# Norms on ScalarE alone: Exp of minus half a Ln in place of Sqrt and a VectorE reciprocal

## Chip, core and metric

One core of a Trainium2 chip. The metric is the device time of one execution in microseconds, the median of several runs.

## What is computed

Two layers of a hybrid trunk on 256 tokens (128 of a context and 128 of a sample), width 1024, all in fp32. Layer 0 is a Mamba-2 SSD mixer beside grouped attention, layer 1 a gated linear attention (GLA). Behind each mixer comes a mixture of 16 experts (top group, then top 2 in it). Five RMS norms stand ahead of mixers and experts and at the end, one more in the SSD mixer, and one per head in the GLA mixer:

```python
def rms_norm(x, w):
    xf = x.astype(F32)
    y = xf * lax.rsqrt(jnp.mean(xf * xf, axis=-1, keepdims=True) + EPS)
    return (y * w.astype(F32)).astype(x.dtype)
# layer: x += gate * mixer(modulate(rms_norm(x)));  x += gate * moe(modulate(rms_norm(x)))
# SSD: y = rms_norm(y * silu(z), norm_w);   GLA: y = rms_norm(y_f + y_b, norm_w) * silu(r), 256 channels a head
```

## The kernel before

Each engine has its own program, and all order between them is by semaphores written out by hand. Activations lie transposed: features on the 128 partitions, 8 tiles (KT), by 256 tokens (T). SyncE streams some 290 MB of weights in tiles of 1 MB through 6 ring slots, and 12 slots in the expert stages; `slot_used` frees them in the order of their use. TensorE multiplies tile by tile; its fp32 matmuls appear in the trace as two instructions each. Banks of PSUM (`ps`) are reused by hand.

A main norm, `norm(i)` for i = 0 to 4, runs so: ScalarE squares the 8 tiles into `hT` (L923); TensorE sums them over the features with a matrix of 1/1024 into bank 0 (semaphore `ss`); ScalarE takes the root with epsilon as bias into `rstd` (L926, semaphore `rms`); VectorE inverts it (L1176) and scales 16 half tiles (L1185, or 8 whole tiles at L1181 for i = 4); ScalarE adds the shift to each (L935), and TensorE starts on the first tiles as they come. norm(0) also needs the first modulation row, which ScalarE copies (L916) once eight weight tiles have been used.

The SSD norm: ScalarE squares the gated result (L997); TensorE sums it into bank 0; ScalarE takes the root (L999, `yrms`). TensorE waits for `yrms` before it writes attention scores over bank 0, with three matmuls for the rotary embedding (`C(ROT)`) between. VectorE's part (`ssd_norm`, L1277 and eight times L1279) comes later, between the maxima of the second group of scores (L1305 to L1313) and the normalising of its exponentials (L1321), which ScalarE computes meanwhile (L1008, L1010).

The GLA norm: ScalarE squares (L1063); TensorE sums per head into banks 4 and 5 (`gss` after each bank, two heads a bank); ScalarE takes the root of each bank, 128x512 (L1066, `grms`); VectorE inverts one head at a time (L1407), scales (L1408) and gates (L1409, `gyn`) its two tiles. The output projection on TensorE waits for both banks' `grms` and for each tile's `gyn`.

ScalarE evaluates its functions from tables, and the build puts an ACT_TABLE_LOAD ahead of an activation whose function the active table lacks. Such loads are in no line of the source: they carry the line of the activation that follows. Square, Copy and Identity need none. Where an activation has one wait, the wait is the activation's own, and the load ahead of it does not wait; where it has two (L926: `set_up` and `ss`), the load waits for `ss`. Other functions around the norms: Exp and Ln for dt (L940, L943), Exp of the segments (L983), Exp of the softmax (L1008), Exp in the router (L1070, L1072), Silu in projections and experts (L1038, L1094).

```python
act.wait_ge(S("ss"), i + 1)
act.activation(rstd[:, 0, :], ps[:, 0, 0:T], ACT.Sqrt, bias=eps[:, :]).then_inc(S("rms"), 1)
# VectorE
dve.wait_ge(S("rms"), i + 1)
step(dve.reciprocal(rstd[:, 0, :], rstd[:, 0, :]))
```

Of the kernel before, what the change touches and what calls it, by code (L numbers as in the profile page):

```python
# [19 lines left out]
ACT = mybir.ActivationFunctionType  # L20
# [6 lines left out]
T = 256  # L27
# [15 lines left out]
PER_EXPERT = 6  # L43
# [58 lines left out]
def build(nc, A, O):  # L102
    with ExitStack() as ctx:
# [21 lines left out]
        rstd = sb("rstd", [P, GH, T])  # L125
# [20 lines left out]
        eps = sb("eps", [P, 1])  # L146
# [114 lines left out]
        def _(sp):  # L261
# [24 lines left out]
            for l in range(2):  # L286
                for j in range(len(IN[l])):
                    w_in_load(l, j)
                    for c in ada_after(l, j):
                        ada(3 * l + 1 + c // KT, c % KT)  # L290
                for j in range(n_out[l]):
                    if l == 0:
                        ada(3, j)
                    n = pos["out", l, j]
                    wait_free(n)
                    load(n, w_out[l][256 * j:256 * j + 256, :].rearrange("(k p) n -> p k n", p=P), 2)
                base = pos["moe", l]
                wgu = [A[w][l].rearrange("e (p k) f -> p e k f", p=P) for w in ("w_gate_exp", "w_up_exp")]
                wd = A["w_down_exp"][l].rearrange("e (p j k) d -> p e j k d", p=P, k=2)

                def expert(e, c, n):

                    if c < 4:
                        src = wgu[c // 2][:, bass.ds(e, 1), 4 * (c % 2):4 * (c % 2) + 4, :]
                        return slot(n, 4), src.rearrange("p a k f -> p (a k) f")
                    src = wd[:, bass.ds(e, 1), c - 4, :, :]
                    return slot(n, 2), src.rearrange("p a k d -> p (a k) d")

                for n, (a, c) in enumerate(PAIR_ORDER):
                    wait_free(base + n)  # L310
                    if n == 0:
                        sp.wait_ge(*((S("gy_raw"), 2) if l else (S("att_raw"), 3)))
                    if MOE_SLOT[n] == RING + 4:
                        sp.wait_ge(*((S("gyn"), KT) if l else (S("slot_used"), pos["out", 0, KT // 2 - 1] + 1)))
                    if MOE_SLOT[n] == RING + 5:
                        sp.wait_ge(S("slot_used"), pos["out", l, n_out[l] - 1] + 1)
                    dst, src = expert(a, c, base + n)
                    sp.dma_start(dst, src).then_inc(S(f"landed{home[base + n]}"), 16)
                with sp.Fori(1, PAIRS) as i:
                    for n, (a, c) in enumerate(PAIR_ORDER):  # L320
                        sp.wait_ge(S("slot_used"), i * (2 * PER_EXPERT) + (base + n + 1 - 2 * PER_EXPERT))
                        dst, src = expert(i * 2 + a, c, base + n)
                        sp.dma_start(dst, src).then_inc(S(f"landed{home[base + n]}"), 16)

                sp.wait_ge(S("need"), l + 1)
                most = sp.value_load(need[0:1, l:l + 1], min_val=0, max_val=T)
                with sp.If(most > CAP):
                    sp.wait_ge(S("slot_used"), base + NE * PER_EXPERT)
                    with sp.Fori(0, NE) as e:
                        with sp.Fori(1, T // CAP) as r:  # L330
                            it = e * (T // CAP - 1) + r
                            for c in range(PER_EXPERT):

                                sp.wait_ge(S(f"o{l}_used"), it * PER_EXPERT + (c + 1 - PER_EXPERT))
                                dst, src = expert(e, c, c)
                                assert home[c] == c
                                sp.dma_start(dst, src).then_inc(S(f"o{l}_landed{c}"), 16)

                    sp.wait_ge(S(f"o{l}_used"), (NE * (T // CAP - 1) + 1) * PER_EXPERT)
            for s in range(NS):  # L340
# [58 lines left out]
        def _(pe):  # L399
# [302 lines left out]
            def moe(l):  # L702
# [123 lines left out]
                with pe.If(most > CAP):  # L826
                    pe.sem_inc(S(f"o{l}_used"), PER_EXPERT)
                    with pe.Fori(0, NE) as e:
                        with pe.Fori(1, T // CAP) as r:
                            it = e * (T // CAP - 1) + r  # L830

                            def wait(n):
                                pe.wait_ge(S(f"o{l}_landed{n}"), it * 16)

                            def mark(ins):
                                ins.then_inc(S(f"o{l}_used"), 1)
                            pe.wait_ge(S(f"o{l}_v"), it * O_STEPS + (1 - O_STEPS))
                            for k in range(KT):
                                for s in range(NS):
                                    last = mm(pe, ps[:, 0, k * CAP:(k + 1) * CAP], xtok[:, s, k * P:(k + 1) * P],  # L840
                                              O_DISP[:, s * CAP:(s + 1) * CAP], s == 0, s == 1)
                            last.then_inc(S(f"o{l}_p"), 1)
                            for s in range(NS):
                                last = mm(pe, ps[0:CAP, 1, tk(s)], O_DISW[:, s * CAP:(s + 1) * CAP], C(IDENT), True, True)
                            last.then_inc(S(f"o{l}_p"), 1)
                            pe.wait_ge(S(f"o{l}_v"), it * O_STEPS + (3 - O_STEPS))
                            gate_or_up(2, [O_HG], 0, wait, mark)
                            gate_or_up(3, [O_HG], 2, wait, mark)
                            pe.wait_ge(S(f"o{l}_v"), it * O_STEPS + (4 - O_STEPS))
                            for f in range(FT):  # L850
                                last = mm(pe, ps[:, 1, f * CAP:(f + 1) * CAP], O_ACT[:, f * P:(f + 1) * P], cst[0:CAP, IDENT, 0:CAP], True, True)
                            last.then_inc(S(f"o{l}_p"), 1)
                            pe.wait_ge(S(f"o{l}_v"), it * O_STEPS + (5 - O_STEPS))
                            down(2, [O_HT], 4, wait, mark)
                            pe.wait_ge(S(f"o{l}_v"), it * O_STEPS)
                            for m in range(KT):
                                last = mm(pe, ps[:, 4 + m // 2, (m % 2) * T:(m % 2 + 1) * T], O_YS[:, m * P:(m + 1) * P],
                                          O_CT, False, False, shared=True)
                            last.then_inc(S(f"o{l}_p"), 1)
# [24 lines left out]
        def _(act):  # L884
# [33 lines left out]
            def norm(i):  # L918
# [4 lines left out]
                    act.activation(hT[:, k, :], xT[:, k, :], ACT.Square).then_inc(S("sq"), 1)  # L923
                act.wait_ge(S("set_up"), 1)
                act.wait_ge(S("ss"), i + 1)
                act.activation(rstd[:, 0, :], ps[:, 0, 0:T], ACT.Sqrt, bias=eps[:, :]).then_inc(S("rms"), 1)  # L926
                if i == 0:
                    ada_copy(0)
                if i < 4:
# [7 lines left out]
            def even():  # L937
# [58 lines left out]
                act.wait_ge(S("y_gated"), 2)  # L996
                act.activation(W(4), zsf, ACT.Square).then_inc(S("ysq"), 1)  # L997
                act.wait_ge(S("yss"), 1)
                act.activation(rstd[:, 1, :], ps[:, 0, 0:T], ACT.Sqrt, bias=eps[:, :]).then_inc(S("yrms"), 1)  # L999
                for g in range(3):  # L1000
                    nh, w = (8, 256) if g else (16, 128)
                    act.wait_ge(S("negm"), g + 1)
# [21 lines left out]
            def odd():  # L1024
# [38 lines left out]
                act.activation(W(3), yaf, ACT.Square).then_inc(S("gsq"), 1)  # L1063
                for b in range(2):
                    act.wait_ge(S("gss"), b + 1)
                    act.activation(rstd[:, 2 * b:2 * b + 2, :].rearrange("p h t -> p (h t)"), ps[:, 4 + b, :], ACT.Sqrt, bias=eps[:, :]).then_inc(S("grms"), 1)  # L1066

            def moe(l):
                act.wait_ge(S("g_sub"), l + 1)
# [63 lines left out]
        def _(dve):  # L1133
# [38 lines left out]
                    step(scales(l, *((8, NMIX) if t == 0 else (32, NFFN))))  # L1172

            def norm(i):
                dve.wait_ge(S("rms"), i + 1)
                step(dve.reciprocal(rstd[:, 0, :], rstd[:, 0, :]))  # L1176
                if i == 0:
                    ada_done(0)
                for k in range(KT):
# [21 lines left out]
            def even():  # L1201
# [72 lines left out]
                    tt(zs[:, :, tk(s)], zs[:, :, tk(s)], xbc[:, 0:KT, tk(s)], ALU.mult).then_inc(S("y_gated"), 1)  # L1274
                def ssd_norm():
                    dve.wait_ge(S("yrms"), 1)
                    step(dve.reciprocal(rstd[:, 1, :], rstd[:, 1, :]))  # L1277
                    for k in range(KT):
                        last = stt(zs[:, k, :], zs[:, k, :], feat[:, SSDN + k:SSDN + k + 1], rstd[:, 1, :], ALU.mult, ALU.mult)  # L1279
                        if k < KT - 1:  # L1280
                            step(last)
                    last.then_inc(S("yssd"), 1)
# [53 lines left out]
            def odd():  # L1336
# [65 lines left out]
                    dve.tensor_copy(yatt[:, :, tk(s)], ps[:, 2 * s:2 * s + 2, :].rearrange("p b (k t) -> p (b k) t", k=4)).then_inc(S("gy"), 1)  # L1402
                dve.wait_ge(S("proj_free"), 28)
                for i in range(KT):
                    if i % 2 == 0:
                        dve.wait_ge(S("grms"), i // 4 + 1)
                        step(dve.reciprocal(rstd[:, i // 2, :], rstd[:, i // 2, :]))  # L1407
                    step(stt(yatt[:, i, :], yatt[:, i, :], feat[:, GLAN + i % 2:GLAN + i % 2 + 1], rstd[:, i // 2, :], ALU.mult, ALU.mult))  # L1408
                    tt(yatt[:, i, :], yatt[:, i, :], zs[:, i, :], ALU.mult).then_inc(S("gyn"), 1)  # L1409
                dve.wait_ge(S("slot_used"), pos["out", 1, n_out[1] - 1] + 1)  # L1410
# [163 lines left out]
```

## Time and profile before

| | |
|---|---|
| median of 3 runs | 1195.73 us (1193.99 to 1200.53) |
| profiled execution | 1196.1 us, its span 1194.0 us |
| TensorE busy | 1036.6 us (87%), mean granted clock 0.917 |
| VectorE busy | 269.9 us (23%) |
| ScalarE busy | 198.6 us (17%) |
| data moved by DMA | 302.84 MB |

Times in the rows are microseconds from the start of the span. Busy time of an engine says how much it works, the chain of waits what the end waited for. An idle stretch in brackets, with the name behind the arrow, says how long the engine stood still before an instruction and what released it. The granted clock is a share of full speed: 1.00 is 2.4 GHz, 0.50 is 1.2 GHz.

### The profile page before, as it was taken

The numbers are of one execution on the slowest core, as the hardware profiler recorded it, in microseconds if no ns is written. First come the engines' busy times: TensorE is split into PE (matmuls) and PEld (weight loads), VectorE is DVE, ScalarE is ACT, GpSimd is POOL, SyncE is SP. The second block draws the span as 40 slices with busy tenths as digits, with TensorE's granted clock in tenths as the row PEclk, the third lists the DMA queues.
The fourth block names the chain that finished last, engine by engine and source line by source line (L and its number), as shares of the span: only waits on it lengthen the run. The fifth ranks groups of instructions, "written<-read, shape, count | busy, mean of one in ns | idle before, by whom it ended". The sixth has DMA issues, their size and how long they took to land.

```text
span 1194.0 us, 12914 instructions
## 1 busy us (share of the span) xinstructions
PE 1036.6 (87%) x5318; PEld 662.9 (56%) x5318; DVE 269.9 (23%) x531; ACT 198.6 (17%) x402; POOL 33.4 (3%) x34
## 2 busy tenths in 40 slices
PE   0799998773399789999999799978988899999995
PEld 0477776453377554455554377746976545555433
DVE  0346003735400430010000400037144310010003
ACT  0310213323200420000000300122013200010002
POOL 5000101200000000000000000000000000000000
PEclk9789999987699879999999899987588899999998
DMA  9758775100057719999999558831037199999980
GB/s 306 276 192 273 254 259 209 36 1 1 0 183 311 282 41 423 421 422 422 422 422 415 194 199 310 289 135 36 1 141 282 71 423 421 422 422 422 422 351 36
DMA packets 75521, 302.84 MB, mean 254 GB/s; under 512 B 5261, under 2 KB 40855, under 8 KB 44759
## 3 DMA queue, kind: packets, MB, share of 16 engines
q1 hardware_dynamic: 67232, 294.67, 63.2%
q10 hardware_dynamic: 7479, 6.74, 1.7%
q0 software_dynamic: 768, 0.83, 0.4%
q8 instruction: 32, 0.52, 0.2%
q14 instruction: 10, 0.08, 0.0%
HBM read 298.81 MB, written 3.41 MB: 253 GB/s over the span
## 4 chain that ended last, share of the span: by engine, by line
PE 82%; DVE 8%; ACT 3%; DMA 2%; issue 2%; POOL 1%; ACTq 0%; POOLq 0%; DVEq 0%
PE ps L255 79%; PE ps L404 3%; DMA xtok<-in_x_sample_dram 2%; ACT wide L1008 1%; ACT hT L935 1%; POOL mix L393 1%; DVE rstd L1176 1%; DVE tiny L1305 1%; DMA ring<-in_w_ada_dram 1%; ACTq L886 0%; DVE wide L1476 0%; DVE wide L1474 0%; DVE mix L1279 0%; DVE wide L1330 0%; ACT L926 0%
## 5 line engine op out<-in xcount | busy, mean ns | idle before, releaser
L255 PE MATMUL ps<-ring,wide 128*64 128x512 f32 x768 | 171.3, 594 | 1.5 <-ACT wide L1098 1.5
L255 PE MATMUL ps<-mix,wide 128*64 128x512 f32 x768 | 168.0, 592 | 0.0
L255 PE MATMUL ps<-hT,ring 128*128 128x256 f32 x640 | 146.2, 387 | 0.0
L255 PEld LDWEIGHTS ps<-hT,ring 128*128 128x128 f32 x640 | 122.1, 193 | 30.1 <-ACT mix L954 6.7
L255 PEld LDWEIGHTS ps<-mix,wide 128*64 128x64 f32 x768 | 55.0, 137 | 108.8 <-issue 108.8
L255 PEld LDWEIGHTS ps<-ring,wide 128*64 128x64 f32 x768 | 54.0, 137 | 107.1 <-issue 105.2
L255 PE MATMUL ps<-wide 128*128 (+4 forms) x512 | 87.4, 344 | 6.9 <-DVE wide L1265 3.3
L255 PE MATMUL ps<-mix,ring 128*128 128x256 f32 x384 | 85.3, 381 | 1.0 <-DVE mix L1409 1.0
L255 PEld LDWEIGHTS ps<-wide 128*128 128x128 f32 (+1 forms) x512 | 74.6, 194 | 16.3 <-DVE wide L1265 4.1
L255 PEld LDWEIGHTS ps<-mix,ring 128*128 128x128 f32 x384 | 72.2, 190 | 17.5 <-issue 8.1
L255 PEld LDWEIGHTS ps<-wide,xtok 128*128 128x128 f32 x512 | 63.7, 206 | 18.3 <-issue 11.4
L255 PE MATMUL ps<-wide,xtok 128*128 (+1 forms) x512 | 66.8, 293 | 6.3 <-DVE wide L1476 6.3
L1496 DVE TENSOR_TENSOR wide<-wide,ps 128x512 f32<-128x512 f32 x16 | 16.8, 1052 | 213.3 <-PE ps L255 213.3
L255 PE MATMUL ps<-ring,hT 128*128 128x256 f32 x256 | 57.4, 382 | 0.0
L404 PE MATMUL ps<-cst,wide 128*128 128x128 f32 x172 | 27.7, 312 | 32.4 <-DVE wide L1325 29.8
L255 PEld LDWEIGHTS ps<-ring,hT 128*128 128x128 f32 x256 | 48.0, 190 | 12.9 <-issue 1.7
L255 PE MATMUL ps<-ring,csilu 128*32 128x512 f32 x384 | 50.2, 612 | 2.9 <-DMA ring<-in_w_ada_dram 2.2
L1488 DVE COPY wide<-ps 128x512 f32<-128x512 f32 x16 | 11.1, 691 | 160.9 <-PE ps L255 160.9
L1166 DVE TENSOR_TENSOR mods<-ps,feat 128x32 f32<-128x32 f32 x6 | 1.1, 190 | 193.1 <-PE ps L404 193.1
L404 PEld LDWEIGHTS ps<-cst,wide 128*128 128x128 f32 x172 | 23.7, 164 | 35.1 <-issue 24.0
L1194 DVE SCALAR_TENSOR_TENSOR xT<-ps,mods,xT 128x128 f32<-128x128 f32 x64 | 19.9, 347 | 97.5 <-PE ps L255 86.0
L1081 ACT ACTIVATE wide<-ps 128x512 f32<-128x512 f32 x16 | 9.6, 597 | 155.9 <-PE ps L255 155.9
(230 smaller groups left out, 830.2 us busy)
## 6 DMA issues: line engine op xcount, KB each, us to landing
mix<-in_w_gate_exp_dram SPq DMA_DIRECT2D x64, 1024.0 KB, 14.4
ring<-in_w_up_exp_dram SPq DMA_DIRECT2D x64, 1024.0 KB, 17.5
ring<-in_w_ada_dram SPq DMA_DIRECT2D x48, 1024.0 KB, 7.4
ring<-in_w_down_exp_dram SPq DMA_DIRECT2D x32, 1024.0 KB, 12.5
mix<-in_w_down_exp_dram SPq DMA_DIRECT2D x32, 1024.0 KB, 14.7
ring<-in_w_in_even_dram SPq DMA_DIRECT2D x16, 1024.0 KB, 6.0
ring<-in_w_in_odd_dram SPq DMA_DIRECT2D x12, 1024.0 KB, 7.9
ring<-in_w_out_even_dram SPq DMA_DIRECT2D x8, 1024.0 KB, 5.6
```

What stands on the lines that cost most here:

```text
L255: return pe.matmul(out, lhsT, rhs, start=first, stop=last, skip_group_check=shared)
L393: pool.tensor_tensor(heads(U), C(GE if n % 2 else LE)[:, None, :].broadcast_to([P, HEADS, P]), tiny[:, a0:a0 + 16][:, :, None].broadcast_t ...
L404: return pe.transpose(out, in_, cst[0:n, IDENT, 0:n])
L935: act.activation(hT[:, k, tk(s)], hT[:, k, tk(s)], ACT.Identity, bias=mods[:, l, c + k, s:s + 1]).then_inc(S("h_ready"), 1)
L1008: act.activation(pr[:, h, :], sc[:, h, :], ACT.Exp, scale=SCALE, bias=tiny[:, NEGM + h:NEGM + h + 1], accum_out=tiny[:, RSUM + h:RSUM + h ...
L1081: act.activation(W(1)[:, 0:512], ps[:, 0, :], ACT.Copy).then_inc(S("hg"), 1)
L1166: tt(mods[:, l, 16 * t:16 * t + 16, :].rearrange("p (j b) s -> p j b s", b=4), ps[:, ADA_TURN[third], :].rearrange("p (b j r) -> p j b r", ...
L1176: step(dve.reciprocal(rstd[:, 0, :], rstd[:, 0, :]))
L1194: last = stt(xT[:, k, tk(s)], ps[:, 4 + k // 2, (k % 2) * T + s * P:(k % 2) * T + (s + 1) * P], mods[:, l, c + k, s:s + 1], xT[:, k, tk(s) ...
L1305: step(dve.tensor_reduce(tiny[:, MX:MX + nh], sc, AX.X, ALU.max))
L1488: dve.tensor_copy(YS[:, 512:1024], ps[:, 1, :]).then_inc(S("ys"), 1)
L1496: tt(HACT.rearrange("p (f a) -> p a f", f=FT), SIL.rearrange("p (a f) -> p a f", f=FT), ps[:, 3, :].rearrange("p (a f) -> p a f", f=FT), A ...
```

## The change

In each norm the root becomes a Ln of the same input with the same bias, and a second activation, Exp with scale -0.5, gives the inverse root; VectorE's reciprocals go (10 of them). Exp waits for Ln by a semaphore (`rms` itself, `yln`, `gln`). What other engines wait for (`rms`, `yrms`, `grms`) is set by Exp. In the GLA norm the second bank's Ln comes after the first bank's Exp. Apart from the norms, the branch for experts with more than 64 tokens waits on one semaphore for its six weight tiles in place of six.

```diff
--- before.py
+++ after.py
@@ -334,7 +334,7 @@
                                 sp.wait_ge(S(f"o{l}_used"), it * PER_EXPERT + (c + 1 - PER_EXPERT))
                                 dst, src = expert(e, c, c)
                                 assert home[c] == c
-                                sp.dma_start(dst, src).then_inc(S(f"o{l}_landed{c}"), 16)
+                                sp.dma_start(dst, src).then_inc(S(f"o{l}_landed"), 16)
 
                     sp.wait_ge(S(f"o{l}_used"), (NE * (T // CAP - 1) + 1) * PER_EXPERT)
             for s in range(NS):
@@ -830,7 +830,8 @@
                             it = e * (T // CAP - 1) + r
 
                             def wait(n):
-                                pe.wait_ge(S(f"o{l}_landed{n}"), it * 16)
+                                if n == 0:
+                                    pe.wait_ge(S(f"o{l}_landed"), it * (16 * PER_EXPERT))
 
                             def mark(ins):
                                 ins.then_inc(S(f"o{l}_used"), 1)
@@ -923,7 +924,9 @@
                     act.activation(hT[:, k, :], xT[:, k, :], ACT.Square).then_inc(S("sq"), 1)
                 act.wait_ge(S("set_up"), 1)
                 act.wait_ge(S("ss"), i + 1)
-                act.activation(rstd[:, 0, :], ps[:, 0, 0:T], ACT.Sqrt, bias=eps[:, :]).then_inc(S("rms"), 1)
+                act.activation(rstd[:, 1, :], ps[:, 0, 0:T], ACT.Ln, bias=eps[:, :]).then_inc(S("rms"), 1)
+                act.wait_ge(S("rms"), 2 * i + 1)
+                act.activation(rstd[:, 0, :], rstd[:, 1, :], ACT.Exp, scale=-0.5).then_inc(S("rms"), 1)
                 if i == 0:
                     ada_copy(0)
                 if i < 4:
@@ -996,7 +999,9 @@
                 act.wait_ge(S("y_gated"), 2)
                 act.activation(W(4), zsf, ACT.Square).then_inc(S("ysq"), 1)
                 act.wait_ge(S("yss"), 1)
-                act.activation(rstd[:, 1, :], ps[:, 0, 0:T], ACT.Sqrt, bias=eps[:, :]).then_inc(S("yrms"), 1)
+                act.activation(rstd[:, 2, :], ps[:, 0, 0:T], ACT.Ln, bias=eps[:, :]).then_inc(S("yln"), 1)
+                act.wait_ge(S("yln"), 1)
+                act.activation(rstd[:, 1, :], rstd[:, 2, :], ACT.Exp, scale=-0.5).then_inc(S("yrms"), 1)
                 for g in range(3):
                     nh, w = (8, 256) if g else (16, 128)
                     act.wait_ge(S("negm"), g + 1)
@@ -1063,7 +1068,10 @@
                 act.activation(W(3), yaf, ACT.Square).then_inc(S("gsq"), 1)
                 for b in range(2):
                     act.wait_ge(S("gss"), b + 1)
-                    act.activation(rstd[:, 2 * b:2 * b + 2, :].rearrange("p h t -> p (h t)"), ps[:, 4 + b, :], ACT.Sqrt, bias=eps[:, :]).then_inc(S("grms"), 1)
+                    two = rstd[:, 2 * b:2 * b + 2, :].rearrange("p h t -> p (h t)")
+                    act.activation(two, ps[:, 4 + b, :], ACT.Ln, bias=eps[:, :]).then_inc(S("gln"), 1)
+                    act.wait_ge(S("gln"), b + 1)
+                    act.activation(two, two, ACT.Exp, scale=-0.5).then_inc(S("grms"), 1)
 
             def moe(l):
                 act.wait_ge(S("g_sub"), l + 1)
@@ -1172,8 +1180,7 @@
                     step(scales(l, *((8, NMIX) if t == 0 else (32, NFFN))))
 
             def norm(i):
-                dve.wait_ge(S("rms"), i + 1)
-                step(dve.reciprocal(rstd[:, 0, :], rstd[:, 0, :]))
+                dve.wait_ge(S("rms"), 2 * (i + 1))
                 if i == 0:
                     ada_done(0)
                 for k in range(KT):
@@ -1274,7 +1281,6 @@
                     tt(zs[:, :, tk(s)], zs[:, :, tk(s)], xbc[:, 0:KT, tk(s)], ALU.mult).then_inc(S("y_gated"), 1)
                 def ssd_norm():
                     dve.wait_ge(S("yrms"), 1)
-                    step(dve.reciprocal(rstd[:, 1, :], rstd[:, 1, :]))
                     for k in range(KT):
                         last = stt(zs[:, k, :], zs[:, k, :], feat[:, SSDN + k:SSDN + k + 1], rstd[:, 1, :], ALU.mult, ALU.mult)
                         if k < KT - 1:
@@ -1402,9 +1408,7 @@
                     dve.tensor_copy(yatt[:, :, tk(s)], ps[:, 2 * s:2 * s + 2, :].rearrange("p b (k t) -> p (b k) t", k=4)).then_inc(S("gy"), 1)
                 dve.wait_ge(S("proj_free"), 28)
                 for i in range(KT):
-                    if i % 2 == 0:
-                        dve.wait_ge(S("grms"), i // 4 + 1)
-                        step(dve.reciprocal(rstd[:, i // 2, :], rstd[:, i // 2, :]))
+                    dve.wait_ge(S("grms"), i // 4 + 1)
                     step(stt(yatt[:, i, :], yatt[:, i, :], feat[:, GLAN + i % 2:GLAN + i % 2 + 1], rstd[:, i // 2, :], ALU.mult, ALU.mult))
                     tt(yatt[:, i, :], yatt[:, i, :], zs[:, i, :], ALU.mult).then_inc(S("gyn"), 1)
                 dve.wait_ge(S("slot_used"), pos["out", 1, n_out[1] - 1] + 1)
```

The changed order on ScalarE, with the table loads that the build puts in. First norm(1), ahead of the first expert stage. Before:

```order
L923 ACTIVATE hT<-xT 128x256 x8
L926 ACT_TABLE_LOAD
L926 ACTIVATE rstd<-ps,eps 128x256
L935 ACTIVATE hT<-hT,mods 128x128 x16
L1070 ACT_TABLE_LOAD
L1070 ACTIVATE tiny<-tiny 128x8
L1072 ACTIVATE tiny<-tiny 128x8
```

Now:

```order
L924 ACTIVATE hT<-xT 128x256 x8
L927 ACT_TABLE_LOAD
L927 ACTIVATE rstd<-ps,eps 128x256
L929 ACT_TABLE_LOAD
L929 ACTIVATE rstd<-rstd 128x256
L938 ACTIVATE hT<-hT,mods 128x128 x16
L1078 ACTIVATE tiny<-tiny 128x8
L1080 ACTIVATE tiny<-tiny 128x8
```

The load ahead of the router's Exp (L1070) has moved into the norm, between Ln and Exp.

Next the GLA norm, ScalarE, with the semaphores that are waited for. Before:

```order
L1060 DMA out_dram<-hT 128x4x256 [waits state]
L1060 DMA out_dram<-hT 128x4x256
L1063 ACTIVATE wide<-mix 128x2048 [waits gy]
L1066 ACT_TABLE_LOAD
L1066 ACTIVATE rstd<-ps,eps 128x512 [waits gss] x2
```

Now:

```order
L1068 ACTIVATE wide<-mix 128x2048 [waits gy]
L1072 ACT_TABLE_LOAD
L1072 ACTIVATE rstd<-ps,eps 128x512 [waits gss]
L1074 ACT_TABLE_LOAD
L1074 ACTIVATE rstd<-rstd 128x512 [waits gln]
L1072 ACT_TABLE_LOAD
L1072 ACTIVATE rstd<-ps,eps 128x512 [waits gss]
L1074 ACT_TABLE_LOAD
L1074 ACTIVATE rstd<-rstd 128x512 [waits gln]
```

One load has become four, since the two banks alternate between the functions.

Last, norm(3), which follows the GLA norm on ScalarE. Before:

```order
L1066 ACTIVATE rstd<-ps,eps 128x512 x2
L923 ACTIVATE hT<-xT 128x256 x8
L926 ACTIVATE rstd<-ps,eps 128x256
L935 ACTIVATE hT<-hT,mods 128x128 x16
L1070 ACT_TABLE_LOAD
```

It had no load, because the root's table was active from the GLA norm; now its rows are those shown for norm(1), with two loads. Over the program there are 20 loads before and 26 now.

## Rows read from the trace of the kernel before

**Rows 1.** Page, part 4: the chain that ended last, by engine
```profile
PE 82%; DVE 8%; ACT 3%; DMA 2%; issue 2%; POOL 1%; ACTq 0%; POOLq 0%; DVEq 0%
```
**Rows 2.** The same chain in order of time: start, duration, engine and line
```profile
296.60 1.67 DVE rstd L1277
...
676.48 1.76 DVE rstd L1176
...
1181.59 1.76 DVE rstd L1176
```
**Rows 3.** Timeline, norm(1): start, duration, instructions, idle time before and releaser
```profile
403.24 1.28 ACT L926 ACT_TABLE_LOAD   x1 [0.83 <-PE ps L255]
404.54 0.47 ACT L926 ACTIVATE rstd<-ps,eps 128x256 f32<-128x256 f32 x1
405.11 1.75 DVE L1176 RECIPROCAL rstd<-rstd 128x256 f32<-128x256 f32 x1 [3.15 <-ACT rstd L926]
406.90 5.29 DVE L1185 SCALAR_TENSOR_TENSOR hT<-xT,mods,rstd 128x128 f32<-128x128 f32 x16
```
**Rows 4.** Groups of instructions, ScalarE: busy us, mean ns, idle before
```profile
L923 ACT ACTIVATE hT<-xT 128x256 f32<-128x256 f32 x40 | 15.9, 413 | 64.5 <-DVE xT L1194 54.7 <-DVE xT L1151 9.9
...
L960 ACT ACTIVATE mix<-mix 128x512 f32<-128x512 f32 x6 | 3.7, 624 | 0.0
```
**Rows 5.** Timeline, ScalarE: the awaited copy in norm(0), the router after norm(1)
```profile
49.92 0.60 ACT L916 ACTIVATE ada_row<-ps 128x512 f32<-128x512 f32 x1 [8.74 <-PE ps L255]
...
417.77 0.21 ACT L1070 ACTIVATE tiny<-tiny 128x8 f32<-128x8 f32 x1 [3.55 <-DVE tiny L1429]
```
**Rows 6.** Timeline, SSD norm on ScalarE and the first scores on TensorE
```profile
268.20 0.47 ACT L999 ACTIVATE rstd<-ps,eps 128x256 f32<-128x256 f32 x1 [4.04 <-PE ps L255]
...
268.69 1.28 ACT L1008 ACT_TABLE_LOAD   x1
...
270.67 2.06 PE L255 MATMUL ps<-mix 64*128 64x128 f32 x32
```
**Rows 7.** Timeline, SSD norm on VectorE, beside ScalarE's last exponential
```profile
296.51 1.74 DVE L1277 RECIPROCAL rstd<-rstd 128x256 f32<-128x256 f32 x1
...
298.29 4.13 DVE L1279 SCALAR_TENSOR_TENSOR mix<-mix,feat,rstd 128x256 f32<-128x256 f32 x8
...
300.24 0.24 ACT L1010 ACTIVATE tiny<-tiny 128x8 f32<-128x8 f32 x1
302.34 0.16 DVE L1321 TENSOR_TENSOR tiny<-tiny 128x8 f32<-128x8 f32 x1
```
**Rows 8.** Timeline, GLA norm and the start of its output projection
```profile
867.95 6.50 PE L255 MATMUL ps<-wide,cst 128*128 128x256 f32 x16 [3.26 <-ACT wide L1063]
871.77 0.69 ACT L1066 ACTIVATE rstd<-ps,eps 128x512 f32<-128x512 f32 x1 [2.57 <-PE ps L255]
...
874.35 0.48 DVE L1408 SCALAR_TENSOR_TENSOR mix<-mix,feat,rstd 128x256 f32<-128x256 f32 x1
874.49 0.69 ACT L1066 ACTIVATE rstd<-ps,eps 128x512 f32<-128x512 f32 x1 [2.03 <-PE ps L255]
874.87 0.42 DVE L1409 TENSOR_TENSOR mix<-mix 128x256 f32<-128x256 f32 x1
...
875.44 27.86 PE L255 MATMUL ps<-mix,ring 128*128 128x256 f32 x128 [0.99 <-DVE mix L1409]
```
**Rows 9.** Timeline, norm(3)
```profile
909.89 0.47 ACT L926 ACTIVATE rstd<-ps,eps 128x256 f32<-128x256 f32 x1 [0.85 <-PE ps L255]
...
912.25 5.29 DVE L1185 SCALAR_TENSOR_TENSOR hT<-xT,mods,rstd 128x128 f32<-128x128 f32 x16
```
**Rows 10.** Windows of 2 us: width, busy PE, PEld, DVE, ACT, POOL, clock, DMA
```profile
872.00:874.00 2.00, 2.00 (x7) 1.64 (x6) 1.44 (x1) 0.46 (x1) 0.00 (x0) 0.60 1.04 438
...
910.00:912.00 2.00, 0.00 (x0) 0.00 (x0) 1.54 (x1) 0.36 (x1) 0.00 (x0) 1.00 1.04 438
...
914.00:916.00 2.00, 1.58 (x8) 1.24 (x7) 1.90 (x7) 2.00 (x8) 0.00 (x0) 0.64 1.04 438
```

## The prediction

> **What bounds the kernel now.** I read the chain of waits first: 82% of the span is TensorE, 8% VectorE, 3% ScalarE [rows 1]. So an edit of ScalarE and VectorE work counts only where that chain leaves TensorE. There the chain in order of time names the norms: of the seven places the change touches, the reciprocal of four is seen on the chain in [rows 2] (the SSD norm at 296.60, norm(2) at 676.48, norm(4) at 1181.59) and [rows 3] (norm(1) at 405.11); [rows 8] and [rows 9] show the other two, the GLA norm and norm(3). norm(0) is not there. Then I read the timeline around each norm, since what decides is which wait ends last there.
>
> About 0.5% of this kernel's time, 6 us, is what a measurement can tell from no change.
>
> **The change, part by part.** It takes a DVE reciprocal away (1.75 us for 128x256) and a Sqrt becomes a Ln of the same operands (same duration taken: both are one pass over the same tile). It adds an Exp on ScalarE. The order of the changed kernel shows what the diff does not: Ln and Exp do not share a table, so a load stands ahead of each Exp, and loads rise from 20 to 26.
>
> *One Exp.* The nearest rows are SBUF to SBUF passes: 413 ns for 128x256, 624 ns for 128x512 [rows 4].
>
> *norm(1), norm(2), norm(4).* Before, from the start of the load to the first scaling on VectorE: 403.24 to 406.90, 3.66 us [rows 3]. Now: load 1.28, Ln 0.47, load 1.28, Exp 0.41, with 0.02 between instructions of one engine (404.54 less 403.24 and 1.28) and 0.10 to VectorE (405.11 less 404.54 and 0.47): 3.60. The second load with the Exp costs what the reciprocal cost. Gain 0.06 each, taken as -0.15 for the three. The load of the Exp table that the router needed after norm(1) and norm(3) goes away, at no gain: after it ScalarE sat idle 3.55 us, waiting for VectorE [rows 5]. The same holds for the load ahead of the dt exponential after norm(0); its cover is the projection that runs meanwhile, and without it the gain would be 1.28.
>
> *norm(0).* What TensorE and VectorE wait for there is the copy of the first modulation row at 49.92, ahead of which ScalarE sat idle for 8.74 us behind its root [rows 5]. A load and an Exp, 1.7 us, fit into that: 0. Without that cover it would read like norm(1), -0.06.
>
> *The SSD norm.* ScalarE first. The root's load is already ahead of its wait, the Exp load follows the Ln directly, where it followed the root (268.69 after 268.20 + 0.47), and the Exp ends at 268.69 + 1.28 + 0.02 + 0.41 = 270.40. This is the one place where the semaphore moves past a load that TensorE used to ignore: TensorE may not overwrite bank 0 with scores before it. It starts them at 270.67, after the rotation matmuls [rows 6]. Covered by 0.2 us; were the Exp 0.5 us longer, 0.3 us would show. VectorE then: the reciprocal starts at 296.51, the first of eight scalings at 298.29, and they end at 302.42. Without it they start at 296.51 and end at 300.64. The next wait there is ScalarE's exponentials, which end at 300.48 [rows 7], just before. So the whole 298.29 - 296.51 = 1.78 us is gained: -1.78.
>
> *The GLA norm.* Here the order matters most. The two halves alternate Ln and Exp, so four loads stand where one did, and the first alone is hidden (ScalarE idles 2.57 us after it, until TensorE's sum). The output projection waits for both halves and for the first gated row. Before: the second root ends at 874.49 + 0.69 = 875.18, the row at 875.29, TensorE starts at 875.44 [rows 8]. Now, from 871.77: Ln to 872.46, load to 873.76, Exp (0.62) to 874.40, load to 875.71, Ln to 876.41, load to 877.71, Exp to 878.36, TensorE 0.06 later (as at any ScalarE release) at 878.42. That is +2.98. The four reciprocals that VectorE saves, 7 us, are worth nothing: the rows it feeds are one per 3.5 us of matmuls (27.86/8), and it was ahead before.
>
> *norm(3).* Before, the root found its table still active from the GLA norm: 909.89 to 912.25, 2.36 us [rows 9]. Now the GLA norm leaves Exp active, so both loads are paid, 3.60 us: +1.24.
>
> *TensorE's clock.* The wait ahead of the GLA output projection grows from 1 us to 878.42 - 874.45 = 3.97 us. The nearest row is norm(3), where TensorE was idle from 909.8 to 913.8: the granted clock was 1.00 in the gap and 0.64, then 0.50, in the windows after [rows 10], a fall from 2.4 to 1.2 GHz. A low clock under this very shape costs 6.50 us for 16 matmuls [rows 8], against 16 x 27.86/128 = 3.48 at full clock: 3.0 us for one such stretch. Bounds 0 and 3.0; I take 1.0, nearer the low end, because the fall is not certain and came in norm(3) only after the wait had ended. Norm(3)'s own clock I charge nothing: it is low there already.
>
> The rest of the diff, one semaphore in place of six for the overflow experts, lies in a branch that the traced run does not enter: 0.
>
> **Sum.** -0.15 - 1.78 + 2.98 + 1.24 = +2.29, with the clock +3.3. The profiled execution took 1196.1 (span 1194.0 and 2.1 around it), 0.4 above the median of 1195.7; so 1199.4 for it, and 1199.0 for a median. Shown runs alone reach from 1194.0 to 1200.5.
>
> On the two tables: the changed order has a load between Ln and Exp in every norm. The Trainium skill (ScalarE: Activation LUTs, "Table sets: the hidden batching unit") says that one set holds both exp and ln, so that the pair needs a single load; by it the sum would be 9.1 us lower (rival D). The order of this build does not agree, and I go by the order.
>
> **The rivals.**
> (A) The clock falls in the GLA gap and the projection pays the full 3.0 us or more, or a second stage loses its clock too: 1195.7 + 2.3 + 3.0 = 1201.0, up to 1203 with a second fall of half that. For it: norm(3)'s gap is as long. Against: the clock held at 1.00 through that whole wait.
> (B) Slower, clear of the noise: a load right behind an activation costs more than its row, since the engine would have to empty first. Seven loads on the path stand so (one in each of norms 1 to 4, three in the GLA norm). At one more load's time each, 1.3 us, that is 9.1 us: 1195.7 + 2.3 + 9.1 = 1207. It decides from 0.5 us a load (+3.5, at the 6 us line). Against it: at 268.69 a load began 0.02 us behind a root, and took 1283 ns as everywhere [rows 6]; but no activation there waited right behind it, which leaves a little room. The Trainium skill (ScalarE: Activation LUTs, "What ACT_TABLE_LOAD costs") puts a drain of 1380 ns on top of 1283 ns for each switch; by it this rival would be 9.7 us. The rows at 268.69 and 403.24 to 404.54 show no such drain.
> (C) The clock falls out luckier than in the traced run. It was low until 873 [rows 10], and the 16 matmuls that sum the GLA squares took 6.50 us [rows 8]; at full clock they take 3.48, and the longer wait behind them costs nothing: 1195.7 + 2.3 - 3.0 = 1195.0, or 1196.5 for half of it. Against: nothing in the change bears on the clock there, so it is for single runs rather than for a median.
> (D) The change does not cost what the order says, because Ln and Exp use one table after all: the seven loads that stand between them, or between Exp and the next Ln, on the path go: 1195.7 + 2.3 - 9.1 = 1189. Against it stands the order, which shows those loads in the build.
>
> **How the numbers follow.** Forecast 0.60 (1197.5 to 1201); A 0.18; C 0.15; B 0.05; D 0.02. The range leaves out B, D and the tails of A and C: 1194.5 to 1204. Slower by over 0.5% means above 1201.7: B, half of A, and a little of the forecast's edge, 0.16. Faster by over 0.5%: D and a stray, 0.03. The rest, 0.81, within 0.5%.
>
> **What would show it.** Right: 26 loads of 1283 ns; at norm(1) 3.6 us from the load to the first scaling; at norm(3) the same instead of 2.4; the SSD scalings starting at once behind the maxima; TensorE starting the GLA projection some 6.7 us after the first half's sum, where it took 3.7. Wrong: an idle stretch between a Ln and its load or between a load and its Exp (B), the scores of the SSD stage waiting for ScalarE, or a low clock in the GLA projection for more than 6 us.

## The result, and the profile after

The changed kernel takes 1201.87 us (median of 9 runs, 1198.65 to 1204.52), the kernel before 1195.76 (9 runs, 1193.51 to 1200.53). The ratio is 1.0049, with a 95% interval of 1.0033 to 1.0065: 5.9 us slower, from 3.9 to 7.8. The forecast was 1199.0, 3.3 above before, in a range of 1194.5 to 1204.0. So the sign was right and the size was short by 2.6 us. The median lies above the band that the forecast itself had named (1197.5 to 1201), in that of its rival (A), and on the line between "within 0.5%" and "slower".

The chain of waits of the changed kernel, by engine, against [rows 1]:

```profile
PE 82%; DVE 7%; ACT 4%; DMA 2%; issue 2%; POOL 1%; ACTq 0%; POOLq 0%; DVEq 0%
```

One per cent of it has gone from VectorE to ScalarE, as the edit says. The place is still read best norm by norm. Timeline of norm(1) after (start, duration, instructions, idle time before), for [rows 3]:

```profile
400.99 1.28 ACT L927 ACT_TABLE_LOAD   x1 [0.83 <-PE ps L255]
402.28 0.47 ACT L927 ACTIVATE rstd<-ps,eps 128x256 f32<-128x256 f32 x1
402.77 1.28 ACT L929 ACT_TABLE_LOAD   x1
404.07 0.42 ACT L929 ACTIVATE rstd<-rstd 128x256 f32<-128x256 f32 x1
404.59 3.60 DVE L1192 SCALAR_TENSOR_TENSOR hT<-xT,mods,rstd 128x128 f32<-128x128 f32 x11 [4.88 <-ACT rstd L929]
```

From load to first scaling it takes 404.59 - 400.99 = 3.60 us, where 3.66 were taken. Nothing stands between Ln and load (0.02), or between load and Exp (0.02). Norm(3), for [rows 9]:

```profile
913.28 1.28 ACT L927 ACT_TABLE_LOAD   x1 [0.83 <-PE ps L255]
...
916.88 2.30 DVE L1192 SCALAR_TENSOR_TENSOR hT<-xT,mods,rstd 128x128 f32<-128x128 f32 x7 [4.88 <-ACT rstd L929]
```

3.60 again, where 2.36 were taken: 1.24 lost, because there was no load before. The GLA norm, for [rows 8]:

```profile
869.48 0.69 ACT L1072 ACTIVATE rstd<-ps,eps 128x512 f32<-128x512 f32 x1 [2.57 <-PE ps L255]
870.18 1.28 ACT L1074 ACT_TABLE_LOAD   x1
871.48 0.63 ACT L1074 ACTIVATE rstd<-rstd 128x512 f32<-128x512 f32 x1
872.12 1.28 ACT L1072 ACT_TABLE_LOAD   x1
...
873.42 0.69 ACT L1072 ACTIVATE rstd<-ps,eps 128x512 f32<-128x512 f32 x1
...
874.12 1.28 ACT L1074 ACT_TABLE_LOAD   x1
...
875.42 0.63 ACT L1074 ACTIVATE rstd<-rstd 128x512 f32<-128x512 f32 x1
```

TensorE starts the output projection at 876.15, 6.67 us behind the first bank's sum, where it took 875.44 - 871.77 = 3.67: 3.0 lost. It stood still for 3.96 us of it. And then the projection itself is longer. The chain of waits after, in order of time (start, duration, engine and line, instructions):

```profile
876.15 30.57 PE ps L255 x128
```

against 27.86 in [rows 8], 2.7 more for the same 128 matmuls. The windows of 2 us after (columns as in [rows 10], the clock third from the end) say why:

```profile
872.00:874.00 2.00, 0.18 (x1) 0.00 (x0) 1.72 (x5) 1.97 (x3) 0.00 (x0) 1.00 0.99 418
874.00:876.00 2.00, 0.00 (x0) 0.00 (x0) 1.65 (x5) 1.97 (x3) 0.00 (x0) 0.70 0.05 21
876.00:878.00 2.00, 1.85 (x5) 1.52 (x6) 1.85 (x5) 0.05 (x1) 0.00 (x0) 0.50 0.03 8
878.00:880.00 2.00, 2.00 (x6) 1.64 (x5) 1.52 (x4) 0.00 (x0) 0.00 (x0) 0.50 0.00 0
880.00:882.00 2.00, 2.00 (x7) 1.59 (x7) 0.00 (x0) 0.00 (x0) 0.00 (x0) 0.60 0.00 0
```

The clock fell from 1.00 to 0.50 (2.4 to 1.2 GHz) in the wait, and stayed low for some 5 us of work. The Trainium skill (TensorE: Matmul & The Clock Gate, "Why this matters for your kernels") says that idle gaps between bursts of matmuls bring the low clock back. By that rule the fall is a price of this wait, and the trace agrees.

Last the SSD norm, for [rows 6] and [rows 7], timeline after:

```profile
267.75 0.42 ACT L1004 ACTIVATE rstd<-rstd 128x256 f32<-128x256 f32 x1
...
268.44 2.06 PE L255 MATMUL ps<-mix 64*128 64x128 f32 x32
...
294.29 4.12 DVE L1285 SCALAR_TENSOR_TENSOR mix<-mix,feat,rstd 128x256 f32<-128x256 f32 x8
...
298.33 0.16 DVE L1327 TENSOR_TENSOR tiny<-tiny 128x8 f32<-128x8 f32 x1
```

Exp ends 0.27 us before the scores start: covered. The scalings start at once, and from the maxima (291.47 here, 293.70 before) to the normalising at L1327 it takes 6.86 us in place of 302.34 - 293.70 = 8.64: 1.78 gained, to the hundredth. But on the chain, the matmuls behind it, before:

```profile
304.14 3.34 PE ps L404 x16
307.50 1.30 DVE wide L1330 x2
308.94 1.98 PE ps L255 x32
```

and after:

```profile
300.13 3.66 PE ps L404 x16
303.81 1.30 DVE wide L1336 x2
305.25 3.39 PE ps L255 x32
```

0.32 and 1.41 longer: 1.73 of the 1.78 is given back. The windows show the clock at 0.50 in the wait ahead of this place in both kernels. Before it rose in 306 to 308 (0.75), ahead of the 32 matmuls; after it rose only towards their end (0.50 in 306 to 308, 0.96 in 308 to 310).

Added up, the traces give -0.2 for three norms, -1.78 and +1.73 at the SSD norm, +3.0 and +2.7 at the GLA norm, +1.24 at norm(3), +0.3 in the last norm's sum, which ran at 0.50 for longer: +7.0. The profiled execution shows only 4.8 in its span, since its first part was 2.2 shorter. That arose ahead of the first edited instruction: the stretch of 32 matmuls that begins with norm(0)'s sum started 0.5 earlier and took 5.59 us in place of 7.25. Whether it is chance is open: in the fourteen traces of this document the stretch takes 5.59 in five of the six that have Ln and Exp in norm(0), and in one of the eight that have the root there; the others have 6.99 to 7.74.

### The profile page after: what moved, and what is told of

It reads as the page before. It is cut to its first block, busy times and chain, and to the rows that moved or that the text cites. A ratio compares the mean times of both kernels' runs of the same rounds, so it can differ in the third digit from the quotient of the medians.

```text
span 1198.8 us, 12917 instructions
## 1 busy us (share of the span) xinstructions
PE 1039.3 (87%) x5318; PEld 665.4 (56%) x5318; DVE 252.6 (21%) x521; ACT 210.1 (18%) x416; POOL 33.4 (3%) x34
## 4 chain that ended last, share of the span: by engine, by line
PE 82%; DVE 7%; ACT 4%; DMA 2%; issue 2%; POOL 1%; ACTq 0%; POOLq 0%; DVEq 0%
PE ps L255 80%; PE ps L404 3%; DMA xtok<-in_x_sample_dram 2%; ACT wide L1013 1%; POOL mix L393 1%; DVE tiny L1311 1%; DMA ring<-in_w_ada_dram 1%; ACTq L887 0%; ACT L929 0%; ACT L927 0%; DVE wide L1480 0%; DVE wide L1478 0%; DVE wide L1336 0%; DVE mix L1285 0%; DVE wide L1331 0%
## 5 line engine op out<-in xcount | busy, mean ns | idle before, releaser
L255 PE MATMUL ps<-mix,ring 128*128 128x256 f32 x384 | 88.0, 390 | 4.0 <-ACT rstd L1074 4.0
```

The costliest lines, as they stand in the source:

```text
L255: return pe.matmul(out, lhsT, rhs, start=first, stop=last, skip_group_check=shared)
```

## The experiments

All were timed in five rounds beside the kernel before. Differences in us are the ratio's, times 1195.7, with its 95% interval. As what is asked is where a few microseconds go, the traces' own durations decide where the interval is wide.

**The GLA norm undone.** Edit, on the changed kernel:

```diff
-                    two = rstd[:, 2 * b:2 * b + 2, :].rearrange("p h t -> p (h t)")
-                    act.activation(two, ps[:, 4 + b, :], ACT.Ln, bias=eps[:, :]).then_inc(S("gln"), 1)
-                    act.wait_ge(S("gln"), b + 1)
-                    act.activation(two, two, ACT.Exp, scale=-0.5).then_inc(S("grms"), 1)
+                    act.activation(rstd[:, 2 * b:2 * b + 2, :].rearrange("p h t -> p (h t)"), ps[:, 4 + b, :], ACT.Sqrt, bias=eps[:, :]).then_inc(S("grms"), 1)
...
-                    dve.wait_ge(S("grms"), i // 4 + 1)
+                    if i % 2 == 0:
+                        dve.wait_ge(S("grms"), i // 4 + 1)
+                        step(dve.reciprocal(rstd[:, i // 2, :], rstd[:, i // 2, :]))
```

> The change with the GLA norm put back to root and reciprocal; the other six norms keep Ln and Exp. Theory (the loss is the GLA norm's wait, 3.0 us, and the clock that falls in it, 2.7 us; the rest cancels): -1.8 at the SSD norm, -0.15 at three norms, +1.2 at norm(3), so 0.7 us below the kernel before, up to 1.0 above it if the SSD gain is given back to a low clock. TensorE starts the output projection 3.7 us after the first bank's sum and runs it in 27.9 us. Rival (every load in front of an Exp costs more than its row): four such loads are left on the path, 2 us above before.

Measured: 1195.81, ratio 1.0008 (0.9996 to 1.0020), +1.0 (-0.5 to +2.4). The trace has the projection 3.67 us behind the first sum and at full clock:

```profile
871.88 27.88 PE ps L255 x128
```

So by the middle values 4.9 of the 5.9 us lie in the GLA norm. What is left is at the upper end of the expectation, with the SSD gain given back (transposes 3.66, matmuls 3.37).

**The GLA norm alone changed.** The reverse of the edit above, on the kernel before (with the semaphores of the overflow branch, which does not run, merged as in the change).

> The kernel before with only the GLA norm changed (and the overflow branch's semaphores merged, a branch that does not run). Theory: +3.0 for the wait, +2.7 for the low clock in the projection, +1.3 at norm(3), whose root must now load its table: 7.0 us above before, that is more than the whole change costs. Rival (the clock fell by chance in the traced run): 4.3 above before.

Measured: 1202.37, ratio 1.0054 (1.0040 to 1.0067), +6.5 (+4.8 to +8.0). This one norm costs about as much as the whole change; whether it costs more, as I expected, the intervals (4.8 to 8.0, and 3.9 to 7.8) do not tell. Norm(3) pays one load here, since its root no longer finds its table. TensorE stood still for 4.94 us ahead of the projection, and the clock fell again, as the wait ended (0.87 in 880 to 882, 0.50 in 882 to 884). The chain of its trace:

```profile
881.41 29.57 PE ps L255 x128
```

29.57 where 27.88 is full clock: 1.7 this time, 2.7 in the change. The fall came in both traces, but its price varies, and not with the length of the wait: the longer wait, 4.94 us, paid less than the one of 3.96.

**The wait filled.** On the changed kernel, behind the sums of the GLA norm:

```diff
+                for n in range(8):
+                    mm(pe, ps[:, n % 2, 0:T], C(MEAN_V), W(3)[:, 0:T], True, True)
```

> The change with eight extra matmuls of 128x256 on TensorE between the GLA sums and the output projection, into two banks that nobody reads; they fill the 4 us wait. Theory: the wait stays 4 us but is now work, the clock stays at 1.00 and the projection takes 27.9 us in place of 30.6: 2.7 us below the change, 3.3 above before. Rival (the clock has no part in it and the loss lies in the loads): no gain, about 6 above before, or 2.5 more where the extra matmuls themselves run at the low clock.

Measured: 1199.03, ratio 1.0032 (1.0020 to 1.0043), +3.8 (+2.4 to +5.1), 2.1 less than the change, though the two intervals (2.4 to 5.1, and 3.9 to 7.8) overlap. The trace decides: TensorE starts the projection as late as before the filling (10.49 us from the first sum matmul in both traces), the clock is 1.00, and the projection takes 27.88 again. Chain and windows:

```profile
879.56 27.88 PE ps L255 x128
```

```profile
876.00:878.00 2.00, 2.00 (x10) 1.50 (x8) 1.90 (x6) 1.97 (x3) 0.00 (x0) 1.00 0.79 332
878.00:880.00 2.00, 0.52 (x3) 0.44 (x3) 1.59 (x4) 1.45 (x2) 0.00 (x0) 1.00 0.03 12
```

The start is the same, the matmuls are the same, and the clock is what differs: it is the cause of the 2.7 us, and work that computes nothing takes them back.

**The SSD norm alone changed.** The change's two edits at L999 and L1277, on the kernel before (with the unused semaphores merged again).

> The kernel before with only the SSD norm changed (and the same unused semaphores merged). Theory: the eight scalings start 1.8 us earlier and the second softmax group with them. If the clock does not mind, 1.8 us below before. Rival: the traced change gave it back in the matmuls right behind (3.39 us for 32 of them where 1.98 were taken before); if that is the rule, within 0.3 of before.

Measured: 1196.28, ratio 0.9997 (0.9986 to 1.0009), -0.4 (-1.7 to +1.1). The rival is nearer: in the trace the scalings start early and the 32 matmuls behind take 3.39. The interval alone does not exclude a gain of 1.7.

**Only the reciprocal moved.** On the kernel before, no Ln and no Exp:

```diff
+                dve.wait_ge(S("yrms"), 1)
+                step(dve.reciprocal(rstd[:, 1, :], rstd[:, 1, :]))
                 done = 0
                 for g in range(3):
```

> The kernel before, root and reciprocal everywhere, with one reciprocal moved: VectorE inverts the SSD norm's root while it waits for the first scores, 20 us ahead of its use. No Exp, no load is added. Theory: VectorE's path is 1.8 us shorter, as with the change, and the clock behind it gives back 1.4 to 1.7 as in all four traces where the scalings started early: within 0.4 us of before. Rival (Ln and Exp themselves bring the slow matmuls): 1.8 us below before.

Measured: 1195.68, ratio 0.9996 (0.9984 to 1.0008), -0.5 (-1.9 to +1.0). Two things follow. The change's gain at the SSD norm needs no Exp: the reciprocal runs at 268.90, in a wait of VectorE's. And the slow matmuls are there too, so they come with the earlier start, and not with Ln or Exp:

```profile
302.60 3.66 PE ps L404 x16
306.28 1.30 DVE wide L1330 x2
307.72 3.38 PE ps L255 x32
```

Eight traces have scalings that start early and nothing that fills these waits (the change, and the runs that undo or fill the GLA norm, change the SSD norm alone, move the reciprocal, load early on the change, group the GLA loads, and the last one below): all show 3.37 to 3.40 for the 32 matmuls. The three with a late start (before, the GLA norm alone, the early load on the kernel before) show 1.98. What decides when the clock rises again was not found.

**The table load ahead of its wait.** In both kernels the load at the main norms comes only after the wait for `ss`, where the activation has a second wait, for `set_up`. This run takes the second wait out of the norms. On the kernel before, and likewise on the change:

```diff
+                if i == 0:
+                    act.wait_ge(S("set_up"), 1)
...
-                act.wait_ge(S("set_up"), 1)
                 act.wait_ge(S("ss"), i + 1)
```

> The kernel before, with ScalarE's wait for the set-up of epsilon taken once at norm(0) in place of at each norm, so that the root has one wait and its table load stands ahead of it. Theory: the load is hidden under TensorE's sum as in the GLA norm, 1.28 us less at norm(1), norm(2) and norm(4), nothing at norm(3), which has no load: 3.8 below before. Rival (a load ahead of a wait still waits): same as before.

> The change with the same edit. Theory: the first of the two loads is hidden at norm(1) to norm(4), 5.1 us below the change, 0.8 above before. Rival: same as the change, 5.9 above before.

Measured: on the kernel before 1191.77, ratio 0.9966 (0.9954 to 0.9979), -4.1 (-5.5 to -2.5); on the change 1197.16, ratio 1.0007 (0.9996 to 1.0018), +0.8 (-0.5 to +2.2), that is 5.1 below the change. Timeline of norm(1) in the first:

```profile
401.87 1.28 ACT L927 ACT_TABLE_LOAD   x1
401.90 0.30 PEld L255 LDWEIGHTS ps<-hT,cst 128*128 128x128 f32 x2 [0.35 <-ACT hT L925]
403.17 0.47 ACT L927 ACTIVATE rstd<-ps,eps 128x256 f32<-128x256 f32 x1
403.74 1.75 DVE L1177 RECIPROCAL rstd<-rstd 128x256 f32<-128x256 f32 x1 [2.34 <-ACT rstd L927]
```

The load now starts at the last square, while TensorE still sums, and ends about half a microsecond after the sum. From the output projection's start to the first shifted tile it takes 75.05 us against 75.87, so 0.82 a norm and not 1.28. The totals agree with the expectations (3.8 and 5.1 less), but not by its mechanism: a norm gives two thirds of what it was said to, three norms 2.5, which is the edge of the interval. Part of the rest can be seen elsewhere on the chain, in 32 matmuls at the start of the first expert stage, before and with the early load:

```profile
430.99 6.55 PE ps L255 x32
```

```profile
429.63 5.30 PE ps L255 x32
```

They take 5.30 to 5.47 us in all five traces that have the load early, and 6.54 to 6.69 in the nine others. With this 1.2 the sum is 3.7. Why they are faster was not tested.

**Two loads in place of four.** On the change, both Ln of the GLA norm first, then both Exp.

> The change with the GLA norm's two Ln together and then its two Exp: two loads in place of four. The second Ln still waits for the second bank's sum, so TensorE starts only 0.6 us earlier than with the change (6.0 us behind the first bank's sum). Theory (a wait of 4.0 us costs 2.7 us of clock): at 3.4 us the clock either falls, 0.6 below the change and 5.3 above before, or holds, 3.3 below the change and 2.6 above before. Rival (each load has a hidden price of 0.5 us or more): at least 1.6 below the change with the projection still at 30.6 us.

Measured: 1202.34 (1197.19 to 1203.44), ratio 1.0052 (1.0037 to 1.0067), +6.2, no better than the change. In the trace TensorE starts 5.97 us behind the first sum, 0.70 earlier than with four loads, and the clock held (1.00 in 874 to 876, projection 27.88): that execution took 1197.19. But TensorE's own wait is hardly shorter, 3.86 us against 3.96, because the second bank's sum followed the first one faster there; so a wait of nearly the same length kept the clock once and lost it once. The four other executions took 1199.67 to 1203.44 at a lower mean clock (0.909 to 0.912 against 0.920). The clock seems to have fallen in most of them; no trace shows it, or where. The trace refutes the hidden price of a load. Whether a clearly shorter wait would save the clock was not tested.

**One wait filled at the SSD norm.** On the kernel with the reciprocal moved, ahead of the second group's transposes (the list is by group):

```diff
+                    for n in range((0, 13, 0)[g]):
+                        mm(pe, ps[:, 7, 0:T], C(ONES), cst[:, COS:COS + 2, :].rearrange("p a b -> p (a b)"), True, True)
                     for i in range(16):
                         if i % 8 == 0:
                             pe.wait_ge(S("probs"), 2 * g + i // 8 + 1)
```

> The kernel with the early SSD reciprocal, and thirteen extra matmuls of 128x256 on TensorE in the one wait of 6.5 us ahead of the second softmax group's transposes, into a bank that is overwritten behind them. Theory (the SSD gain is real and the low clock takes it back): with the clock kept at 1.00 the 16 transposes take about 1.9 us in place of 3.66 and the 32 matmuls behind them 1.98 in place of 3.38: 3.2 us below before. Rival (the slow matmuls come from something else than the clock): no gain, within 0.5 of before.

Measured: 1195.73 (1188.08 to 1196.98), ratio 0.9995 (0.9982 to 1.0009): no gain, as the rival had it. One execution of the eleven took 1188.08 us, at the highest mean clock of them (0.925 against 0.917 to 0.920); it was not traced. The windows of the traced one show why it decides nothing about the cause: the clock was kept at 1.00 until the extra matmuls ended, TensorE then stood still for 2.9 us, and the clock fell in the middle of the transposes:

```profile
302.00:304.00 2.00, 1.09 (x8) 0.86 (x9) 1.94 (x2) 0.01 (x1) 0.00 (x0) 1.00 0.00 0
304.00:306.00 2.00, 1.88 (x8) 1.48 (x8) 0.08 (x1) 1.08 (x2) 0.00 (x0) 0.53 0.00 0
306.00:308.00 2.00, 0.65 (x6) 0.68 (x8) 1.21 (x2) 0.00 (x0) 0.00 (x0) 0.50 0.00 0
```

**All three waits filled.** The kernel before with the set-up wait taken once, the reciprocal moved and the list (22, 13, 18); then the same with Ln and Exp in all norms but the GLA norm's; then the first without extra matmuls.

> Root and reciprocal as before, with ScalarE's set-up wait taken once, the SSD reciprocal early, and extra matmuls in all three waits of the softmax groups (22, 13 and 18). Theory: 3.9 (loads hidden) + 1.8 (SSD) + 1.6 + 1.4 + 3.4 (three groups at full clock) = about 12 us below before, 1184. Rival (the clock falls between the groups all the same, at the copies): 5 to 7 below before.

> The same version with Ln and Exp in the five main norms and the SSD norm, root and reciprocal in the GLA norm only. Theory: a load and an Exp cost what a reciprocal costs, so within 1 us of the version with roots (0.05 less at each main norm). Rival (Ln and Exp cost something that the rows do not show): 2 us or more above it.

> The fastest version without its extra matmuls: root and reciprocal, ScalarE's set-up wait taken once, the SSD reciprocal early. Theory (the extra matmuls act through the clock and bring some 7 us of its 12): 4.0 for the loads and 0.4 for the reciprocal, 1191.3, with the softmax groups' transposes at 3.66 us and the 32 matmuls behind the second at 3.4. Rival (the two other edits together are worth more than each alone): 1187 or less.

Measured: 1183.76 (four executions), ratio 0.9894 (0.9879 to 0.9909), -12.7 (-14.5 to -10.9); with Ln and Exp 1186.57, 0.9923 (0.9909 to 0.9936), -9.2 (-10.9 to -7.7); without extra matmuls 1190.93, 0.9962 (0.9948 to 0.9975), -4.5. The first is 18 us faster than the change. The first and the last differ in the extra matmuls alone, and their intervals are far apart. Windows of 10 us over the softmax groups, with all waits filled:

```profile
294.00:304.00 10.00, 7.08 (x39) 5.70 (x37) 8.46 (x16) 4.93 (x19) 0.00 (x0) 1.00 0.01 2
304.00:314.00 10.00, 7.84 (x82) 7.06 (x82) 4.09 (x6) 1.32 (x5) 0.00 (x0) 1.00 0.01 2
```

and with the reciprocal moved and nothing filled:

```profile
294.00:304.00 10.00, 1.40 (x7) 1.43 (x8) 9.16 (x16) 3.85 (x17) 0.00 (x0) 0.65 0.01 2
304.00:314.00 10.00, 7.76 (x75) 6.95 (x73) 1.33 (x3) 1.68 (x3) 0.00 (x0) 0.67 0.00 0
```

At full clock the transposes behind an advanced softmax take two times 1.1 us in place of 3.66, the 32 matmuls 1.98 in place of 3.38. The chain with all waits filled (the second half of the transposes, then the 32 matmuls):

```profile
302.93 1.11 PE ps L404 x8
...
305.50 1.98 PE ps L255 x32
```

With the scalings as early as in the change, the same matmuls are fast once the clock is kept: so it is the clock that takes the SSD gain back, which the single filled wait had left open. That all of the 1.78 is then kept is read from the chain; no run fills the waits and leaves the reciprocal where it was. The Ln and Exp version came out 3.5 us (by ratio) above the one with roots, against my expectation. Its traced run lost the clock in the second group (3.69 and 3.70 us there), 3.1 us in all, and at norm(3) the first load is exposed by some 0.5 us, where the version with roots has none. Whether the other runs lost the clock there too was not seen; that Ln and Exp alone cost something more is not excluded.

## Why the prediction was right, and where it was short

*norms 1, 2 and 4*, predicted 3.60 us from load to scaling, -0.06 each: 3.60. *norm(3)*, +1.24: +1.24. *norm(0)*, 0: the chain there still runs over the copied row. *Router load*, 0: right, there is nothing in its place on the chain.

*The SSD norm.* Cover of 0.2 us at the scores: 0.27. -1.78 on VectorE: -1.78. The step that failed is the silence behind it: the clock of the matmuls behind the advanced scalings was a term put at nothing, without a reason. I took the gain through to the end, and in [rows 10] I had looked at the clock of the GLA stage alone. The term measured +1.73.

*The GLA norm.* +2.98: +3.00. Exp estimated at 0.41 and 0.62 us: 0.42 and 0.63.

*The clock in the GLA wait*, taken at 1.0 between 0 and 3.0: 2.7 in the change, 1.7 with that norm alone. This is the term that was mis-sized. The nearest row was norm(3), where TensorE stood still for 3.98 us and the clock fell right behind it; going by that row the upper end was due. I argued myself down because the fall there came only after the wait, which is no reason: what counts is at what clock the work behind it runs.

*Rivals.* (A), the full price of the fall, 1201.0, is nearly what happened; it had a chance of 0.18, the forecast itself 0.60. (B), a hidden drain at each load, fell: between Ln, load and Exp the gaps are 0.02 us. The Trainium skill (ScalarE: Activation LUTs, "What ACT_TABLE_LOAD costs") adds a drain to each load; the traces of this kernel do not agree. (C) and (D) did not occur. The 9.1 us of (D) were added up wrongly, though to nearly the right number: with one table the load ahead of norm(3)'s Ln would go as well, 1.3 more, and in the GLA norm the second Ln would still wait for its sum, which ends at 874.45, so that only some 2.5 of the 3.9 could go. The parts that were costed at full clock came to 2.3, as forecast; with 2.7 for the clock at the GLA norm, 1.7 at the SSD norm and 0.3 in the last sum that makes 7.0 in the traces, against 5.9 (3.9 to 7.8) in the runs. So the sum was right in its parts, and short by what the clock took in three places; the total lay inside the range because the range had been made wide enough for (A). In the traced run the shorter first part, which no term of the sum held, hides 2.2 of it.

## What to carry to other kernels

An operation moved from one engine to another is priced by the switches it brings, and where two functions use different tables the order of the built program, not the source, tells how many there are; interleaving them over two buffers doubled them. In this kernel a wait on TensorE's path had a second price, the clock at which the work behind it ran (1.7 to 2.7 us at one place), and a gain of 1.78 on the path was lost to the same: look at the granted clock on both sides of every wait that an edit lengthens or advances. When a wait can't be shortened, harmless matmuls that reach right up to its end can be worth more than the edit (here some 7 us).

## What I had not expected of the hardware

Extra matmuls in three waits bring some 7 us of 1191 (1190.93 to 1183.76); a single fill that ended 2.9 us short of its wait's end brought nothing. With two waits at the activation the table load waited too; with one wait the load ran ahead, worth 4.1 us here in one moved line. And starting a stage 1.8 us earlier made it 1.7 us longer, with the same slow matmuls in all eight traces that have the early start and nothing that fills the waits. Why is open.
